# A linear-attention phase re-ordered: maxima and copies of the cross-attention into waits for roots, states ahead of running sums, outputs of two heads in halves

## The chip, the cores and the metric

The kernel runs on one core of a Trainium2 chip. The core has five engines that run side by side, each through its own list of instructions in order, and meet at semaphores: TensorE (PE, matrix products), VectorE (DVE), ScalarE (ACT), GpSimd (POOL) and SyncE (SP, here for issuing transfers). The metric is the device time of one execution in microseconds; lower is better. The median of three timed runs is given, and one further execution was recorded by the profiler.

## The reference

Two causal layers over 1024 tokens of width 1024. The change is in the token mixer of the first, a gated linear attention with four heads, and in the cross-attention to 256 memory tokens that runs beside it:

```python
def gla_mixer(h, w_in, w_gate2, b_gate, o_norm):
    q, k, v, glr, og, xq = split_cols(h @ w_in, ...)
    log_a = jax.nn.log_sigmoid((glr @ w_gate2 + b_gate).astype(F32)) / GLA_GATE_NORM
    o = chunked_gla(hs(q) * (GLA_DK ** -0.5), hs(k), hs(v), hs(log_a))
    o = rms_norm(o, o_norm).reshape(Bsz, S, D_MIX) * jax.nn.silu(og.astype(F32))
    return o.astype(h.dtype), xq

def chunked_gla(q, k, v, log_a):                  # chunks of 64 tokens
    b = jnp.cumsum(log_a, axis=2)
    att = jnp.einsum('bnihk,bnjhk->bnhij', q * jnp.exp(b - b_ref), k * jnp.exp(b_ref - b))
    o_intra = jnp.einsum('bnhij,bnjhv->bnihv', jnp.where(tril, att, 0.0), v)
    def step(state, xs):
        o = jnp.einsum('bchk,bhkv->bchv', qc, state)
        state = dc[..., None] * state + jnp.einsum('bchk,bchv->bhkv', kc, vc)
    return o_intra + o_inter

def memory_cross_attention(xq, mem_n, w_kv, q_norm, k_norm):
    p = jax.nn.softmax(jnp.einsum('bshd,bmhd->bhsm', q, k) * (XA_HEAD_DIM ** -0.5), axis=-1)
    return jnp.einsum('bhsm,bmhd->bshd', p, v)
```

## The kernel before

Everything is one program in phases: projections, the attention phase here (`gla_phase`), its output projection, a gated MLP, and then a second layer of other kind. At the end of a phase the engines meet at a barrier. Only `gla_phase` is touched. In it each engine has a list written out by hand, head after head; nothing else decides the order.

In a head `h` PE projects the head's queries and keys (`project`: weights split into a high and a low part, eight pieces over the width, each of six products), makes the gate (`gate`), the token products inside pairs of chunks and across a pair (`token_products`), turns the keys (by the identity) and makes the state changes from them (`state_changes`), and last the outputs (`outputs`, from the attention and from the state, eight pairs of chunks). In heads 0 and 1 the projections of the next head lie between; heads 2 and 3 have no such work, and there the cross-attention lies between, in 19 steps. A step `s` (class `CrossUnits`) makes on PE the score of unit `s` (L1996), turns the weights of unit `s - 2` (L2004) and mixes the values of unit `s - 3` (L2013). DVE makes the maximum of the score (L2021), copies the turned weights out of PSUM (L2029), inverts the total, and scales the mixed values (L2036). ACT makes the exponentials (L2048, two of 256 columns). Each waits for the one before it, and score `s` needs the exponentials of `s - 2`, since two banks take turns. The table `CROSS` says at which place of which head the steps stand, the same for the three engines:

```python
CROSS = {(1, "out"): range(0, 3), (2, "att"): range(3, 5), (2, "state"): range(5, 8), (2, "out"): range(8, 11),
         (3, "att"): range(11, 13), (3, "state"): range(13, 16), (3, "out"): range(16, CrossUnits.STEPS)}
```

DVE further makes the running sums of the log gates (`sums_of`: the log, L2371; a scan, L2372; two differences), four products of queries and keys with the gate factors (`product`, 0 to 3), a pair of factors after the cross products (`cross_pair`), the seven states one after the other (`states`, L2427 and L2429) and the scaled outputs (`outputs`, L2438). The outputs need the reciprocal root of their mean square: ACT squares each pair's output (L2350), POOL makes the root for four pairs at once (L2244, L2246). "Root" below means this chain. ACT also copies the attention, the turned keys (L2333) and the projections (`copy`) out of PSUM, makes the softplus of the gate (`gate_in`, `gate_out`), the gate's factors (`factor`) and the high parts of weights (`high`); DVE makes their low parts (`low`, L2366). Four PSUM banks are handed on as a ring: each use waits until the use four places earlier has been read.

## Time and profile before

| | us |
|---|---|
| median of the timed runs | 2525.84 (2524.62 to 2526.7) |
| profiled execution, its own time | 2521.81 |
| its span, first to last instruction | 2520.0 |
| PE busy | 2432.4 (97%) |
| DVE, ACT, POOL busy | 1729.7, 1033.7, 225.7 |
| mean granted TensorE clock | 0.988 |

The phase runs from 216 to 406 us of the span. In the views below, the table of windows gives for each stretch its length and then each engine's busy time with the number of its instructions, in the order PE, PEld (PE's weight loads), DVE, ACT, POOL, then PEclk, the granted clock of TensorE (1.00 is 2.4 GHz, 0.50 is 1.2 GHz), the share of the transfer engines, and GB/s. A row of a timeline has the start, the duration, the engine, the line of the kernel, the operation, what it writes from what, the shapes, and the number of instructions merged into it; in brackets stand the engine's idle time before it and what ended it. On PE a product in 32 bits counts as two. The end of a matrix product is modelled and overlaps the next start, so the time from one piece of work to the next is read from start to start.

### The profile page before, as it was taken

What the parts mean: (1) busy time and instruction counts of PE and PEld (TensorE: products, weight loads), DVE (VectorE), ACT (ScalarE), POOL (GpSimd) and SP (SyncE); (2) the same over time, 40 slices, a digit from 0 to 9 for tenths busy, and PEclk for the clock granted to TensorE, in tenths of its full rate; (3) what the DMA queues carried; (4) which work ended last, traced back from release to release, by engine and by line L of the source; (5) the groups of instructions that cost most, each with busy time, mean ns of one, the idle gap of its engine ahead of it and who ended that gap; (6) DMA issues with size and microseconds to landing.
All of it is one profiled execution on the core that took longest, in us unless ns stands there. A gap on an engine that the chain in (4) does not pass through costs nothing. (4 is left out here: it accounts for less than half of the span.)

```text
span 2520.0 us, 32372 instructions
## 1 busy us (share of the span) xinstructions
PE 2432.4 (97%) x11700; PEld 2055.1 (82%) x11700; DVE 1729.7 (69%) x2908; ACT 1033.7 (41%) x2126; POOL 225.7 (9%) x271
## 2 busy tenths in 40 slices
PE   7999979999999999998999999999899999999998
PEld 7998757888888887777889889887788888888777
DVE  4532564379899888885553562463669999898896
ACT  6433443344444443335434432333334444443443
POOL 1010021000000000041212021122100000000000
PEclk9999988999999999999999999999999999999999
DMA  4330121322222248743102011212532222226764
GB/s 149 89 89 22 39 79 43 100 69 84 76 92 84 75 142 272 262 142 130 51 17 81 35 34 42 60 34 73 168 115 75 85 84 83 77 91 221 280 200 146
DMA packets 207541, 257.72 MB, mean 102 GB/s; under 512 B 38376, under 2 KB 141784, under 8 KB 207384
## 3 DMA queue, kind: packets, MB, share of 16 engines
q1 hardware_dynamic: 203224, 255.65, 31.0%
q8 instruction: 94, 1.54, 0.3%
q10 hardware_dynamic: 4160, 0.02, 0.1%
q14 instruction: 63, 0.52, 0.1%
HBM read 206.54 MB, written 49.09 MB: 101 GB/s over the span
## 5 line engine op out<-in xcount | busy, mean ns | idle before, releaser
L52 PE MATMUL psum<-f_T_lo 128*128 128x512 f32 x616 | 244.6, 397 | 13.0 <-DVE f_T_lo L676 11.9
L53 PE MATMUL psum<-f_T_lo 128*128 128x512 f32 x616 | 241.3, 392 | 0.0
L54 PE MATMUL psum<-f_T_lo 128*128 128x512 f32 x616 | 241.2, 392 | 0.0
L52 PE MATMUL psum<-w_hi,hT_hi 128*128 128x512 f32 x576 | 229.3, 398 | 4.2 <-DVE w_lo L1445 2.5
L54 PE MATMUL psum<-w_hi,hT_lo 128*128 128x512 f32 x576 | 226.3, 393 | 0.0
L53 PE MATMUL psum<-w_lo,hT_hi 128*128 128x512 f32 x576 | 226.1, 393 | 0.0
L52 PEld LDWEIGHTS psum<-f_T_lo 128*128 128x128 f32 x616 | 116.4, 189 | 48.1 <-DVE f_T_lo L676 21.1
L52 PEld LDWEIGHTS psum<-w_hi,hT_hi 128*128 128x128 f32 x576 | 124.8, 217 | 22.4 <-issue 3.9
L54 PEld LDWEIGHTS psum<-w_hi,hT_lo 128*128 128x128 f32 x576 | 125.0, 217 | 17.9
L53 PEld LDWEIGHTS psum<-w_lo,hT_hi 128*128 128x128 f32 x576 | 125.1, 217 | 16.6
L52 PE MATMUL psum<-hT_hi,f_up_hi 128*128 128x512 f32 x352 | 137.4, 390 | 0.4 <-DVE f_up_lo L615 0.4
L54 PE MATMUL psum<-hT_hi,f_up_lo 128*128 128x512 f32 x352 | 137.0, 389 | 0.0
L53 PE MATMUL psum<-hT_lo,f_up_hi 128*128 128x512 f32 x352 | 137.0, 389 | 0.0
L54 PEld LDWEIGHTS psum<-f_T_lo 128*128 128x128 f32 x616 | 116.4, 189 | 25.0
L53 PEld LDWEIGHTS psum<-f_T_lo 128*128 128x128 f32 x616 | 116.4, 189 | 23.1
L52 PE MATMUL psum<-T_hi,f_s_hi 128*128 128x512 f32 x320 | 124.5, 389 | 0.0
L53 PE MATMUL psum<-f_T_lo,f_s_hi 128*128 128x512 f32 x320 | 124.5, 389 | 0.0
L54 PE MATMUL psum<-T_hi,f_s_lo 128*128 128x512 f32 x320 | 124.5, 389 | 0.0
L52 PE MATMUL psum<-T_hi,f_up_hi 128*128 128x512 f32 x320 | 124.5, 389 | 0.0
L53 PE MATMUL psum<-f_T_lo,f_up_hi 128*128 128x512 f32 x320 | 124.5, 389 | 0.0
L54 PE MATMUL psum<-T_hi,f_up_lo 128*128 128x512 f32 x320 | 124.5, 389 | 0.0
L455 ACT ACTIVATE f_T_lo<-f_up_pieces 128x1024 fp32r<-128x1024 f32 (+1 forms) x72 | 67.0, 957 | 119.1 <-PE psum L54 101.9
(416 smaller groups left out, 6087.7 us busy)
## 6 DMA issues: line engine op xcount, KB each, us to landing
raw<-in_ffn_w_up_dram SPq DMA_DIRECT2D x88, 512.0 KB, 4.7
activations<-f_act SPq DMA_DIRECT2D x44, 512.0 KB, 2.6
f_up_pieces<-activations SPq DMA_DIRECT2D x38, 512.0 KB, 4.4
w_raw<-in_b_w_in_dram SPq DMA_DIRECT2D x18, 1024.0 KB, 5.9
f_up_pieces<-in_ffn_w_down_dram SPq DMA_DIRECT2D x20, 512.0 KB, 4.8
x_between<-XY SPq DMA_DIRECT2D x16, 512.0 KB, 5.2
XY<-x_between SPq DMA_DIRECT2D x16, 512.0 KB, 6.5
f_up_pieces<-activations SPq DMA_DIRECT2D x28, 256.0 KB, 3.9
```

The costliest lines, as they stand in the source:

```text
L52: nc.tensor.matmul(out, lhs_hi, rhs_hi, start=start, stop=False)
L53: nc.tensor.matmul(out, lhs_hi, rhs_lo, start=False, stop=False)
L54: return nc.tensor.matmul(out, lhs_lo, rhs_hi, start=False, stop=stop)
L455: nc.scalar.activation(hi, raw, ACT.Copy).then_inc(b_high, 1)
```

## The change

Only the order of instructions inside `gla_phase` changes, and with it the points at which they wait.

- PE, heads 0 and 1: the keys are turned before the last of the eight pieces of the projection, not after it. The state products, which need ACT's copies of them, follow that piece. ACT takes the copies of the keys first, then the high part of the next weight, then the copy of the projection.
- PE, outputs in two halves, with a new place `half` between them: in head 1 scores 0 and 1 stand there, in head 3 step 16. A new place `keys` stands between the turned keys and the state products: step 5 in head 2, step 13 in head 3.
- DVE, all heads: outputs in two halves; in heads 0 and 1 products 2 and 3 of the next head stand between them.
- DVE, heads 2 and 3, written out one by one: the states of head 2 stand before the scan of head 3; cross steps stand between products and output halves.
- ACT, head 2: the gate factors of head 3 stand between the two halves of the squares; the exponentials of steps 3 and 4 stand ahead of the copies of the keys.

The diff, without the parts that only name the new ring entries:

```diff
-        CROSS = {(1, "out"): range(0, 3), (2, "att"): range(3, 5), (2, "state"): range(5, 8), (2, "out"): range(8, 11),
-                 (3, "att"): range(11, 13), (3, "state"): range(13, 16), (3, "out"): range(16, CrossUnits.STEPS)}
+        CROSS = {(1, "half"): range(0, 2), (1, "out"): range(2, 3), (2, "att"): range(3, 5), (2, "keys"): range(5, 6), (2, "state"): range(6, 8),
+                 (2, "out"): range(8, 11), (3, "att"): range(11, 13), (3, "keys"): range(13, 14), (3, "state"): range(14, 16),
+                 (3, "half"): range(16, 17), (3, "out"): range(17, CrossUnits.STEPS)}
...
@@ scalar engine
-                if fresh:
-                    copy(h + 1, 0)
-                    high(2 * h + 3)
+                cross_steps(cross.act, act, h, "att")
                 if h:
                     act.wait_ge(squared, PAIRS * h)
                 for i in range(2):
                     act.wait_ge(mixed, mixes_before(at(h, "keys", i)) + 1)
                     nc.scalar.activation(k_rows[:, 4 * i:4 * i + 4, :], ...)
-                cross_steps(cross.act, act, h, "att")
-                if more:
+                if fresh:
+                    high(2 * h + 3)
+                    copy(h + 1, 0)
+                cross_steps(cross.act, act, h, "keys")
+                if fresh:
                     factor(h + 1, 0)
                     factor(h + 1, 1)
-                cross_steps(cross.act, act, h, "state")
-                if fresh:
                     copy(h + 1, 1)
                 if h + 2 < LAST:
                     high(2 * h + 4)
+                cross_steps(cross.act, act, h, "state")
                 if h:
                     act.wait_ge(rstd_ready, 2 * h)
                 for p in range(PAIRS):
+                    if p == PAIRS // 2:
+                        if more and not fresh:
+                            factor(h + 1, 0)
+                            factor(h + 1, 1)
+                        cross_steps(cross.act, act, h, "half")
                     act.wait_ge(mixed, mixes_before(at(h, "out", p // 2)) + 1)
...
@@ vector engine (logs_of is the log of sums_of, split off)
-            for h in range(GLA_HEADS):
-                more = h + 1 < GLA_HEADS
-                fresh = h + 1 < LAST
+            for h in range(LAST - 1):
                 cross_pair(h)
-                cross_steps(cross.dve, dve, h, "att")
-                if more:
-                    sums_of(h + 1)
-                if fresh:
-                    low(2 * h + 3)
+                logs_of(h + 1)
+                sums_of(h + 1)
+                low(2 * h + 3)
                 states(h)
...
-                if more:
-                    product(h + 1, 1)
-                outputs(h)
-                if more:
-                    product(h + 1, 2)
-                    product(h + 1, 3)
-                if h == 1:
-                    for part in range(2):
-                        dve.wait_ge(parked[part], 16 * LAST)
-                cross_steps(cross.dve, dve, h, "out")
+                product(h + 1, 1)
+                cross_steps(cross.dve, dve, h, "half")
+                outputs(h, 0)
+                product(h + 1, 2)
+                product(h + 1, 3)
+                outputs(h, 1)
+            for part in range(2):
+                dve.wait_ge(parked[part], 16 * LAST)
+            cross_steps(cross.dve, dve, LAST - 2, "out")
+            first, second, third = CROSS[LAST - 1, "out"]
+            cross_pair(LAST - 1)
+            cross_steps(cross.dve, dve, LAST - 1, "att")
+            cross_steps(cross.dve, dve, LAST - 1, "keys")
+            logs_of(LAST)
+            states(LAST - 1)
+            cross.dve(dve, CROSS[LAST - 1, "state"][0])
+            sums_of(LAST)
+            cross.dve(dve, CROSS[LAST - 1, "state"][1])
+            outputs(LAST - 1, 0)
+            product(LAST, 0)
+            cross.dve(dve, first)
+            product(LAST, 1)
+            outputs(LAST - 1, 1)
+            cross.dve(dve, second)
+            product(LAST, 2)
+            product(LAST, 3)
+            cross.dve(dve, third)
+            cross_pair(LAST)
+            cross_steps(cross.dve, dve, LAST, "att")
+            cross_steps(cross.dve, dve, LAST, "keys")
+            states(LAST)
+            cross_steps(cross.dve, dve, LAST, "state")
+            cross_steps(cross.dve, dve, LAST, "half")
+            outputs(LAST, 0)
+            cross.dve(dve, CROSS[LAST, "out"][0])
+            outputs(LAST, 1)
+            cross.dve(dve, CROSS[LAST, "out"][1])
...
@@ tensor engine (turn_keys is the first half of state_changes, split off)
-                if h + 1 < LAST:
-                    project(2 * h + 2, range(EARLY, DC))
+                fresh = h + 1 < LAST
+                if fresh:
+                    project(2 * h + 2, range(EARLY, DC - 1))
                 cross_at(h, "att")
+                turn_keys(h)
+                if fresh:
+                    project(2 * h + 2, range(DC - 1, DC))
+                cross_at(h, "keys")
                 state_changes(h)
                 cross_at(h, "state")
-                if h + 1 < LAST:
+                if fresh:
                     project(2 * h + 3)
-                outputs(h)
+                outputs(h, 0)
                 if h == 1:
                     pe.wait_ge(copied, 2 * LAST)
                     pe.wait_ge(kv_loaded, 16 * len(kv_loads))
+                cross_at(h, "half")
+                outputs(h, 1)
                 cross_at(h, "out")
```

How this stands in the lists of the engines is shown at three places. The first is PE in head 0, around the turned keys (from `gla_k_out`) and the state products (from `gla_k_rows`); the products with `h_hi` and `h_lo` are the projection. Before:

```order
L2499 MATMUL psum<-h_hi,mem_lo 128x512 x4
L2499 MATMUL psum<-h_lo,mem_lo 128x512 x2
L2499 MATMUL psum<-h_hi,mem_lo 128x512 x2
L2532 MATMUL psum<-ident,gla_k_out 128x96 x8
L2539 MATMUL psum<-gla_v,gla_k_rows 96x192 x7
```

In the changed kernel, whose lines have other numbers, on PE at the same place:

```order
L2536 MATMUL psum<-h_hi,mem_lo 128x512 x2
L2569 MATMUL psum<-ident,gla_k_out 128x96 x8
L2536 MATMUL psum<-h_hi,mem_lo 128x512 x2
L2536 MATMUL psum<-h_lo,mem_lo 128x512 x2
L2536 MATMUL psum<-h_hi,mem_lo 128x512 x2
L2578 MATMUL psum<-gla_v,gla_k_rows 96x192 x7
```

One piece of the projection has moved from before the turned keys to between them and the state products.

The second place is DVE at the end of head 1: the scaled outputs (from `gla_rstd`), the products of head 2 and the first maxima (`rank_rows<-psum`). Before:

```order
L2393 TENSOR_TENSOR gla_k_mid<-XY,gla_k_mid 96x1024
L2438 SCALAR_TENSOR_TENSOR XY<-psum,gla_rstd,XY 128x192 x8
L2402 TENSOR_TENSOR gla_decay<-gla_ends 96x8
L2406 TENSOR_TENSOR gla_k_out<-gla_k_mid,gla_ends 96x1024
L2406 TENSOR_TENSOR gla_q_in<-gla_q_mid,gla_ends 96x1024
L2021 TENSOR_REDUCE rank_rows<-psum 128x2 x3
L2029 COPY cross_room<-psum 128x512
```

In the changed kernel on DVE at the same place:

```order
L2406 TENSOR_TENSOR gla_k_mid<-XY,gla_k_mid 96x1024
L2021 TENSOR_REDUCE rank_rows<-psum 128x2 x2
L2451 SCALAR_TENSOR_TENSOR XY<-psum,gla_rstd,XY 128x192 x4
L2415 TENSOR_TENSOR gla_decay<-gla_ends 96x8
L2419 TENSOR_TENSOR gla_k_out<-gla_k_mid,gla_ends 96x1024
L2419 TENSOR_TENSOR gla_q_in<-gla_q_mid,gla_ends 96x1024
L2451 SCALAR_TENSOR_TENSOR XY<-psum,gla_rstd,XY 128x192 x4
L2021 TENSOR_REDUCE rank_rows<-psum 128x2
L2029 COPY cross_room<-psum 128x512
```

Two of the three maxima have moved ahead of the outputs, and the second four outputs behind the two products; the third maximum still stands behind all outputs.

The third place is DVE in head 2, from the scan (from `gla_keep`) and the states (`gla_state`) to the next cross step. Before:

```order
L2371 SCALAR_TENSOR_TENSOR gla_soft<-raw,gla_soft 96x1024
L2372 SCALAR_TENSOR_TENSOR raw<-gla_keep,gla_soft 96x1024
L2377 TENSOR_TENSOR gla_ends<-raw 96x16
L2378 TENSOR_TENSOR gla_soft<-raw 96x1024
L2427 COPY gla_state<-psum 96x192
L2429 SCALAR_TENSOR_TENSOR gla_state<-gla_state,gla_decay,psum 96x192 x6
L2021 TENSOR_REDUCE rank_rows<-psum 128x2
L2029 COPY gla_v<-psum 128x4x128
```

In the changed kernel on DVE at the same place:

```order
L2382 SCALAR_TENSOR_TENSOR gla_soft<-raw,gla_soft 96x1024
L2440 COPY gla_state<-psum 96x192
L2442 SCALAR_TENSOR_TENSOR gla_state<-gla_state,gla_decay,psum 96x192 x6
L2021 TENSOR_REDUCE rank_rows<-psum 128x2
L2029 COPY cross_room<-psum 128x512
L2030 RECIPROCAL rank_rows<-rank_rows 128x2
L2036 TENSOR_TENSOR XY<-psum,rank_rows 128x128
L2385 SCALAR_TENSOR_TENSOR raw<-gla_keep,gla_soft 96x1024
L2390 TENSOR_TENSOR gla_ends<-raw 96x16
L2391 TENSOR_TENSOR gla_soft<-raw 96x1024
```

The scan and the two differences have moved behind the states and one whole cross step.

## Rows read from the trace of the kernel before

**Rows 1.** PE's waits between 215 and 410 us: total, times, longest.

```profile
PE psum L2004 <- DVE cross_room L2029: 7.0, 2, 4.2
PE psum L1996 <- ACT cross_room L2048: 5.9, 1, 5.9
```

**Rows 2.** Windows: length, busy time of each engine, PEclk, DMA share, GB/s.

```profile
248.15:253.09 4.94, 4.94 (x37) 3.43 (x37) 0.00 (x0) 3.72 (x7) 0.00 (x0) 1.00 0.00 0
324.20:338.30 14.10, 14.08 (x45) 8.43 (x46) 3.30 (x6) 8.74 (x17) 4.96 (x3) 0.50 0.30 125
329.20:338.50 9.30, 9.30 (x38) 6.29 (x37) 1.93 (x4) 6.99 (x9) 0.07 (x2) 0.50 0.00 0
345.70:352.50 6.80, 4.44 (x25) 2.91 (x25) 6.51 (x16) 4.44 (x15) 0.00 (x0) 1.00 0.01 2
367.40:372.80 5.40, 5.32 (x20) 4.21 (x20) 2.54 (x7) 1.47 (x7) 0.00 (x0) 0.50 0.00 0
400.70:405.80 5.10, 4.39 (x21) 4.26 (x21) 1.51 (x5) 0.00 (x0) 0.00 (x0) 0.50 0.00 0
311.50:405.80 94.30, 77.47 (x428) 61.05 (x426) 56.04 (x121) 39.38 (x134) 23.09 (x22) 0.84 0.15 55
```

**Rows 3.** PE's timeline in head 0, up to the next projection.

```profile
253.09 0.72 PE L2499 MATMUL psum<-h_hi,mem_lo 128*128 128x512 f32 x2
...
258.69 0.82 PE L2532 MATMUL psum<-ident,gla_k_out 96*128 96x96 f32 x8
...
261.38 2.49 PE L2539 MATMUL psum<-gla_v,gla_k_rows 128*96 128x192 f32 x14 [1.87 <-ACT gla_k_rows L2333]
...
263.57 0.76 PE L2499 MATMUL psum<-h_hi,mem_lo 128*128 128x512 f32 x2
```

**Rows 4.** DVE's timeline there: the low part of the next weight.

```profile
261.00 1.21 DVE L2366 TENSOR_TENSOR mem_lo<-kv_room,mem_lo 128x1024 fp32r<-128x1024 f32 x1
```

**Rows 5.** PE's timeline: outputs of head 1 and first cross scores.

```profile
311.53 0.81 PE L2551 MATMUL psum<-gla_v,gla_att 128*128 128x192 f32 x4
...
316.43 1.88 PE L1996 MATMUL psum<-kv_room,xqT 128*128 128x512 f32 x4
...
324.22 2.08 PE L1996 MATMUL psum<-kv_room,xqT 128*128 128x512 f32 x2 [5.91 <-ACT cross_room L2048]
```

**Rows 6.** ACT's timeline there: last square of head 1, first exponential.

```profile
316.95 0.32 ACT L2350 ACTIVATE gla_k_rows<-psum 128x192 f32<-128x192 f32 x1
...
323.15 0.47 ACT L2048 ACTIVATE cross_room<-psum,rank_rows 128x256 f32<-128x256 f32 x1 [5.78 <-DVE rank_rows L2021]
```

**Rows 7.** DVE's timeline there: second four outputs, a product, two maxima.

```profile
318.78 1.39 DVE L2438 SCALAR_TENSOR_TENSOR XY<-psum,gla_rstd,XY 128x192 f32<-128x192 f32 x4 [1.23 <-POOL gla_rstd L2246]
...
320.16 1.21 DVE L2406 TENSOR_TENSOR gla_k_out<-gla_k_mid,gla_ends 96x1024 f32<-96x1024 f32 x1
...
322.43 1.28 DVE L2021 TENSOR_REDUCE rank_rows<-psum 128x2 f32<-128x512 f32 x2
```

**Rows 8.** Timelines of DVE, then PE: sums, states and cross steps of head 2.

```profile
343.56 2.29 DVE L2372 TENSOR_TENSOR_SCAN raw<-gla_keep,gla_soft 96x1024 f32<-96x1024 f32 x1
...
347.12 0.35 DVE L2427 COPY gla_state<-psum 96x192 f32<-96x192 f32 x1
...
350.78 0.68 DVE L2029 COPY gla_v<-psum 128x512 f32<-128x512 f32 x1
...
351.61 0.63 PE L2004 MATMUL psum<-ident,cross_room 128*128 128x128 f32 x4 [1.56 <-DVE gla_v L2029]
...
352.91 1.08 PE L1996 MATMUL psum<-kv_room,xqT 128*128 128x512 f32 x2
...
355.10 0.87 PE L2551 MATMUL psum<-gla_v,gla_att 128*128 128x192 f32 x4
```

**Rows 9.** Timelines of DVE and PE where one phase ends and the next begins.

```profile
405.18 0.29 DVE L2036 TENSOR_TENSOR XY<-psum,rank_rows 128x128 f32<-128x128 f32 x1 [1.41 <-PE psum L2013]
...
405.80 1.94 PE L1317 MATMUL psum<-ident,XY 128*128 128x128 f32 x8 [0.65 <-PEq L2064]
```

More of the change, by code:

```diff
@@ L2162, in gla_phase @@
             enter("keys", "act", 2, h)
+            enter_cross(h, "keys")
             enter("delta", "state", 4, h)
             enter_cross(h, "state")
-            enter("out", "dve", 4, h)
+            enter("out", "dve", 2, h)
+            enter_cross(h, "half")
+            enter("out_end", "dve", 2, h)
             enter_cross(h, "out")
@@ L2184, in at @@
         def at(h, kind, i=0):
+            if kind == "out" and i >= 2:
+                return entry_of[h, "out_end"] + i - 2
             return entry_of[h, kind] + i
@@ L2431, in states, with outputs @@
                     dve.wait_ge(state_ready, (PAIRS - 1) * h + p + 1)
-            def outputs(h):
-                for p in range(PAIRS):
+            def outputs(h, half):
+                for p in range(half * PAIRS // 2, (half + 1) * PAIRS // 2):
                     if p % (PAIRS // 2) == 0:
-                        dve.wait_ge(rstd_ready, 2 * h + 1 + p // (PAIRS // 2))
+                        dve.wait_ge(rstd_ready, 2 * h + 1 + half)
                     y = Y[:, p, h * DV:(h + 1) * DV]
@@ L2443, in _ @@
             dve.wait_ge(kept, 2)
+            logs_of(0)
             sums_of(0)
@@ L2449, in _ @@
             product(0, 3)
-            for h in range(GLA_HEADS):
-                more = h + 1 < GLA_HEADS
-                fresh = h + 1 < LAST
+            for h in range(LAST - 1):
                 cross_pair(h)
-                cross_steps(cross.dve, dve, h, "att")
-                if more:
-                    sums_of(h + 1)
-                if fresh:
-                    low(2 * h + 3)
+                logs_of(h + 1)
+                sums_of(h + 1)
+                low(2 * h + 3)
                 states(h)
-                cross_steps(cross.dve, dve, h, "state")
-                if more:
-                    product(h + 1, 0)
+                product(h + 1, 0)
@@ L2463, in _ @@
                 if h + 2 < LAST:
                     low(2 * h + 4)
-                if more:
-                    product(h + 1, 1)
-                outputs(h)
-                if more:
-                    product(h + 1, 2)
-                    product(h + 1, 3)
-                if h == 1:
-                    for part in range(2):
-                        dve.wait_ge(parked[part], 16 * LAST)
-                cross_steps(cross.dve, dve, h, "out")
+                product(h + 1, 1)
+                cross_steps(cross.dve, dve, h, "half")
@@ L2524, in token_products, with turn_keys @@
                 mm.then_inc(mixed, 1)
-            def state_changes(h):
+            def turn_keys(h):
                 pe.wait_ge(factored, h + 1)
@@ L2533, in state_changes @@
                     mm.then_inc(mixed, 1)
+            def state_changes(h):
                 for p in range(PAIRS - 1):
@@ L2542, in state_changes, with outputs @@
                         mm.then_inc(mixed, 1)
-            def outputs(h):
+            def outputs(h, half):
                 pe.wait_ge(masked, h + 1)
-                for p in range(PAIRS):
+                for p in range(half * PAIRS // 2, (half + 1) * PAIRS // 2):
                     i = at(h, "out", p // 2)
```

3 lines of the change are left out of this document (2 added, 1 removed).

## The prediction, made before the changed kernel was run

> **What bounds the kernel now.** I read the waits of TensorE (PE) first. The kernel is PE's: over most of it PE runs without a gap, and only one stretch, the gated linear attention from 216 to 406 us, which the change touches, has large waits: 5.9 us once before a cross-attention score, 4.2 and 2.8 us before turns of the weights [rows 1], and 1.87 us in each of heads 0 and 1 before the state products [rows 3]. Then I read the granted clock. After each of the three long waits PE is granted 0.50, its lower level of 1.2 GHz, and stays there for 14.08, 5.32 and 4.39 us of busy time; the other stretches of the table have 1.00 [rows 2]. At half rate these cost half their busy time, 11.9 us. So from the outputs of head 1 to the end of the phase, 311.5 to 405.8, 94.3 us are 77.5 busy [rows 2], of which 65.6 would be left at full rate, 11.9 for the low clock, and 16.8 of waiting. These last two are what a new order can win: 28.7 us, beside 3.7 in heads 0 and 1.
>
> **Why PE waits there.** The 5.91 us before 324.22 [rows 5]: PE has made scores 0 and 1, and score 2 needs ScalarE's (ACT) exponentials of score 0, which need VectorE's (DVE) maximum. DVE, in order, first finishes head 1: it waits for the root, scales four outputs from 318.78, makes two products, and reaches the maxima at 322.43 [rows 7]; the exponentials start 0.72 later and score 2 1.07 after that [rows 5, 6]. The 4.2 and 2.8 us are the same at heads 2 and 3: a copy of turned weights stands behind the root, the outputs and, in head 2, the products.
>
> **Heads 0 and 1.** The keys are turned at 258.69, ACT first has a copy and a weight part to do, and the state products start at 261.38 [rows 3]. After, the keys are turned one piece of projection earlier. Four pieces take 5.60 (253.09 to 258.69), one 1.4, so they are turned at 257.3, take 0.8, and the last piece fills PE to 259.5, while ACT, now with the keys first, has copied them by 258.8. State products: 259.5 to 261.7 (2.19). The next projection needs the low weight part, which DVE still makes at 261.00 behind the running sums, 1.2 long [rows 4]; ACT gives its high part by 260.7, so that doesn't delay it. PE starts at about 262.3 in place of 263.57. A 1.87 wait goes, one of 0.6 comes: **1.29 us per head, 2.6 for two.** ACT's copy of the projection moves behind the weight part and ends at 261.6, still before PE asks for it; SP's store of it stands behind a load that waits for the low part anyway. DVE's second four outputs now come two products, 2.4 us, later; PE has half a projection and a gate, 5.6 and 1.9, to do before it wants their banks: nothing, and at most 2.4 each if that cover were gone.
>
> **Head 1 into head 2**, on the old time axis less 2.6. Outputs take 4.90 [rows 5]: first half 308.95 to 311.2, scores 0 and 1 to 313.1, second half to 315.7. DVE takes the maximum of score 0 at 312.4, ACT the exponentials at 313.1, so they are out at 314.15, before PE asks for them at 315.7. The wait of 5.91 is gone, and with it the fall of the clock behind it. What is late next: the second root. The last squares start at 316.2, DVE's outputs 1.83 later [rows 6, 7] at 318.0, the maximum of score 2 behind them at 319.35, its exponentials at 320.1 to 321.0, and behind these, in order on ACT, the gate of head 3, whose first two activations (1.4) free the bank that PE's last token products want. PE has turned weights 0 and made gate and token products, 4.94 us together with the last [rows 2], and stands there at 320.9: a wait of 1.5.
>
> **Heads 2 and 3.** A full step of cross-attention is 2.19 of PE, and DVE needs 0.64 for a maximum (two in 1.28 [rows 7]) and about as much for a copy, 0.83 from a copy's start to the next turn [rows 8]; so DVE keeps pace unless something stands in front of it. I walked the new order with these lengths; the waits left on PE:
> - 1.2 us at score 5: ACT ends gate, two attention copies, the softplus and its table loads (6.99 busy in the like stretch [rows 2]) before the exponentials of step 3, now ahead of the key copies; they start at 328.95, PE stands at 328.9.
> - 0.8 at turn 5: seven states and a maximum, 3.66 together (347.12 to 350.78 [rows 8]), stand before the copy of step 6. The states now precede the scan, 3.56 with what follows it [rows 8], so the scan no longer holds them up; it delays step 7 instead, 0.4 at the outputs of head 2.
> - 0.9 at mix 5: step 7's exponentials end at 343.6, the four squares behind them at 345.0, so DVE's first root comes at 346.4 and the bank at 347.15.
> - 1.35 at turn 7 behind one product (1.2 [rows 7]), and 1.7 at turn 8 behind the second product and four outputs (1.39).
> - 1.15 in four small ones, the largest 0.5 at the outputs of head 3, which wait for the first root there.
> - 1.95 at the end: PE is done at 381.7, DVE's last outputs, behind the root of the last squares, at 383.05, the last cross output at 383.35, and the next phase 0.3 later, as 405.80 stands to 405.47 now [rows 9].
>
> Together with the 1.5: 10.95 us. None is longer than 1.7. Gaps of 1.87 in heads 0 and 1 left the clock at 1.00, and so did 345.7 to 352.5, where PE is busy for 4.44 of 6.80 us [rows 2]; the gaps before a fall were 2.8 and more. So I take no fall before the end of the phase. Cold start of the next phase: as before.
>
> One rule of the Trainium skill speaks against this. Its page "TensorE: Matmul & The Clock Gate", section "A second HAM failure mode: psum-queue depth-cycling", says that a PE which idles often for short times between groups of products can swing between both rates and pay again and again. By it the sum would be that of the first rival below. This trace doesn't agree in the one like stretch it has, just named.
>
> **Sum.** Before: 65.6 + 16.8 + 11.9 = 94.3. After by this balance: 65.6 + 10.95 = 76.5, a gain of 17.8, with heads 0 and 1 20.4. Walked from start to start, the phase ends at 383.65 in place of 405.80, a gain of 22.15: the balance counts as work the drain of the last product before each of nine waits, some 0.2 each, and the walk forgets small delays. I take the middle, **21.3 us**. Against the profiled execution, 2521.81, that is 2500.5. The median of the timed runs is 4.0 above it, 2525.84, and becomes **2504.5**. No instruction is added or taken out, table loads included; only the order differs.
>
> **Rivals.**
> 1. *The clock falls in the new gaps* (0.25). The weakest place is 343 to 354, four gaps of 4.3 us together and the engine about half busy, sparser than the one stretch that kept its clock. For: the three falls now each followed a sparse stretch; against: each had one gap of 2.8 or more. Price: the three low stretches cost 7.0, 2.7 and 2.2 us now; the new waits would swallow 1 or 2 of it. One fall costs 2 to 6, two up to 9: 2506.5 to 2513.5. The rule of the Trainium skill's page named above would give this.
> 2. *Waits I counted too short* (0.06): ACT is in order, and the squares of head 2 stand behind exponentials of step 7. If the scan comes a step late, root, outputs and copies of three steps follow, each 1 to 3 us: gain of 12 to 15, 2511 to 2514.
> 3. *The change doesn't reach the wait* (0.03): the half outputs ask for the copies of the projection and the loaded keys before score 0. If one of them is late, the 5.9 stays. Against it: the copy ends at about 310.2, the keys land long before. Then only heads 0 and 1 are won: 2523, same.
> 4. *Slower* (0.03): PE falls to half rate at the first new gap and the sparse order never lets it rise. Some 54 us of the 65.6 of work come after that point; at half rate they take 54 more, of which the waits left, 9, are covered. It decides from the point where the low rate lasts for more than some 30 us of work (21 won and 9 covered); held to the end it costs 45 and gives 2549.5. Against it: the longest low stretch now is 14.1 us, and work of the same kind ended it.
>
> **Numbers.** 0.63 for the forecast, with a range of its own of 2502 to 2507 (balance and walk, and small delays). Beyond about 0.2%, 5 us, a time can be told from no change here. Forecast, rival 1 and rival 2 are all faster by more: 0.94; the same 0.03; slower 0.03. The range runs from 2501, the walk's 2503.7 less what a warmer start of the next phase could save of its first work (1.94 at low clock [rows 9] and what follows), to 2512, most of rival 1, leaving out about 0.15.
>
> **What would show it.** In the changed profile: no wait over 2 us on PE between 311 and 380, granted clock 1.00 throughout; state products of heads 0 and 1 without a wait, the projection after them waiting 0.6 for DVE; exponentials of score 0 between the squares of head 1; waits of 1 to 2 us at the cross token products of head 2, at score 5, and at turns 7 and 8; the next phase's first PE instruction near 383.7. It is wrong if the clock shows 0.50 anywhere there, if a gap exceeds 3 us, or if the phase ends after 390.

## The result, and the profile after the change

The changed kernel's median is 2504.84 us (9 runs, 2496.31 to 2511.73), that of the kernel before 2523.99 in the same session (9 runs): a ratio of 0.9928, with a 95% interval of 0.9915 to 0.9941. Its profiled execution took 2497.09, with a span of 2495.3 and a mean granted clock of 0.992. The phase runs from its first PE instruction at 216.91 to the next phase's at 385.70, 168.79 long; before it was 188.64 (217.16 to 405.80 [rows 9]), so 19.85 were won in it. The other 5 of the profile's difference lie outside it, and runs of one kernel differ by more than that (below).

PE's waits in the phase (total, times, longest), which answer to [rows 1]:

```profile
PE psum L2004 <- DVE gla_v L2029: 2.5, 2, 1.5
...
PE psum L2004 <- DVE cross_room L2029: 1.6, 2, 1.0
...
PE psum L2536 <- DVE mem_lo L2378: 1.2, 3, 0.4
PE psum L2013 <- DVE XY L2451: 1.0, 1, 1.0
PE psum L2554 <- DVE XY L2451: 0.6, 1, 0.6
```

The 5.9 at a score is gone, and the 4.2 and 2.8 at turns with it; inside the phase no wait is longer than 1.5, and 1.77 stands at its end. The windows from head 1's outputs to the end, around the token products of head 2, and over head 2's outputs answer to [rows 2] (columns as there):

```profile
308.64:385.70 77.06, 68.93 (x427) 55.30 (x426) 57.22 (x121) 38.39 (x134) 23.82 (x22) 0.96 0.18 68
319.24:326.36 7.12, 6.96 (x35) 5.41 (x35) 3.54 (x6) 5.96 (x12) 6.26 (x4) 0.54 1.02 416
346.78:357.40 10.62, 7.14 (x44) 4.80 (x43) 9.06 (x21) 5.65 (x23) 2.66 (x4) 1.00 0.00 1
```

PE's busy time fell from 77.47 to 68.93 because less of it is at half rate. One fall of the clock is left, at 319.24, where the prediction has none; over 346.78 to 357.40, where its first rival saw the weakest place, PE works 7.14 of 10.62 us and the clock is 1.00. PE's timeline, in head 0 (as [rows 3]), from head 1's outputs into head 2 (as [rows 5]) and at the end (as [rows 9]):

```profile
257.08 0.82 PE L2569 MATMUL psum<-ident,gla_k_out 96*128 96x96 f32 x8
...
259.16 2.44 PE L2578 MATMUL psum<-gla_v,gla_k_rows 128*96 128x192 f32 x14
262.02 0.74 PE L2536 MATMUL psum<-h_hi,mem_lo 128*128 128x512 f32 x2 [0.42 <-DVE mem_lo L2378]
...
308.64 0.81 PE L2590 MATMUL psum<-gla_v,gla_att 128*128 128x192 f32 x4
...
310.92 1.88 PE L1996 MATMUL psum<-kv_room,xqT 128*128 128x512 f32 x4
...
319.24 3.19 PE L2554 MATMUL psum<-gla_q_mid,gla_k_mid 96*128 96x128 f32 x16 [0.65 <-DVE XY L2451]
322.59 1.97 PE L2559 MATMUL psum<-gla_q_in,gla_k_out 96*64 96x64 f32 x16 [0.16 <-ACT gla_soft L2284]
...
329.91 0.63 PE L2004 MATMUL psum<-ident,cross_room 128*128 128x128 f32 x4 [1.03 <-DVE gla_v L2029]
...
385.70 1.07 PE L1317 MATMUL psum<-ident,XY 128*128 128x128 f32 x8 [1.77 <-PEq L2064]
```

State products start without a wait, and the next projection waits 0.42 for the low part. The 1.03 at 329.91 was not predicted. What made it stands in the timelines of POOL and DVE there:

```profile
311.94 0.19 POOL L2251 TENSOR_SCALAR gla_sums<-gla_sums 128x4 f32<-128x4 f32 x1 [20.25 <-ACT gla_k_rows L2362]
...
316.27 0.95 POOL L2251 TENSOR_SCALAR gla_sums<-gla_sums 128x4 f32<-128x4 f32 x1 [3.05 <-ACT gla_k_rows L2362]
...
324.47 2.35 POOL L1118 TENSOR_TENSOR h_lo<-o_w_stage,h_hi 128x1024 fp32r<-128x1024 f32 x1
...
315.96 1.21 DVE L2419 TENSOR_TENSOR gla_q_in<-gla_q_mid,gla_ends 96x1024 f32<-96x1024 f32 x1
...
324.60 2.77 DVE L2430 TENSOR_TENSOR gla_q_in<-gla_q_in,gla_ends 96x512 f32<-96x512 f32 x1 [3.58 <-PE psum L2559]
```

DVE's product at 324.60 takes 2.77; the same line takes 0.69 in other heads. It ends 0.55 after POOL's split of the output weights (326.82), nearly as if it had only started there. And POOL's first step of the second root takes 0.95 in place of 0.19: it ends at 317.22, 0.05 after DVE's product does.

### The profile page after: what moved, and what is told of

Its sections match the earlier page's. It is cut to its first block and busy times, and to the rows that moved or that the text cites. A ratio compares the mean times of both kernels' runs of the same rounds, so it can differ in the third digit from the quotient of the medians.

```text
span 2495.3 us, 32379 instructions
## 1 busy us (share of the span) xinstructions
PE 2423.2 (97%) x11700; PEld 2049.3 (82%) x11700; DVE 1731.1 (69%) x2908; ACT 1033.1 (41%) x2126; POOL 226.0 (9%) x271
```

## The experiments

Three stretches tell the kernels apart: from the phase's first PE instruction to head 1's outputs, from there to head 2's outputs, and from there to the next phase. They are differences of start times in PE's timeline of each profile; falls are the places in the phase at which the granted clock drops to 0.50 (0 to 3: in that head; 1 into 2: between its outputs and the next head's products).

| kernel | to head 1's outputs | to head 2's outputs | to the next phase | phase | falls (head) |
|---|---|---|---|---|---|
| before | 94.37 | 43.57 | 50.70 | 188.64 | 1 into 2, 2 into 3, end |
| changed | 91.73 | 32.86 | 44.20 | 168.79 | 2 |
| early keys alone | 91.64 | 40.20 | 50.25 | 182.09 | 1 into 2, 2, 2 into 3, end |
| halves alone | 96.03 | 37.01 | 50.66 | 183.70 | 0, 2, 2 into 3, end |
| sums ahead of states | 91.69 | 37.42 | 45.65 | 174.76 | 2 (twice), 3 |
| head 3 uncut | 91.67 | 32.39 | 47.53 | 171.59 | end |
| changed, again | 91.68 | 32.45 | 47.19 | 171.32 | 2, 3 |
| splits moved | 91.72 | 31.43 | 44.20 | 167.35 | none |
| product behind | 94.59 | 36.27 | 44.19 | 175.05 | 0, 2 (twice) |
| splits and product | 94.50 | 30.65 | 47.16 | 172.31 | 1, 3 |
| splits moved, again | 91.73 | 31.62 | 44.20 | 167.55 | 2 |
| gate twice | 106.78 | 32.56 | 44.19 | 183.53 | start, 0, 1, 2 |
| filler | 93.56 | 31.42 | 45.06 | 170.04 | none |
| gate early | 91.76 | 31.58 | 44.19 | 167.53 | 2 |

**Early keys alone**, on the kernel before:

```diff
-                    project(2 * h + 2, range(EARLY, DC))
+                    project(2 * h + 2, range(EARLY, DC - 1))
                 cross_at(h, "att")
-                state_changes(h)
+                turn_keys(h)
+                if h + 1 < LAST:
+                    project(2 * h + 2, range(DC - 1, DC))
+                state_changes(h)
```

(on ACT the key copies come first, then the weight part and the copy, as in the change)

> The kernel before with one part of the change: in heads 0 and 1 PE turns the keys one piece ahead of the end of the projection, and ACT copies them ahead of the weight part and of the projection's copy. Theory (the term of 1.29 per head): the wait of 1.87 before the state products goes, one of about 0.5 for VectorE's low weight part comes; head 1's outputs start 2.6 us earlier than the 311.53 of before, and all that follows keeps its length, the 5.9 wait included. Median about 2.6 below before, 2521. Rival: the low part decides alone when the next projection starts, and nothing is won: outputs start at 311.5. Rival: the key copies moved ahead delay the weight's high part and the low part with it, and it is slower by up to 1 per head.

Ratio 0.9989 (0.998 to 0.9999). Head 1's outputs come 2.73 earlier; both rivals fall. What follows is not as long as before, though its order is the same: PE's timeline at the 5.9 wait, and the windows behind it:

```profile
321.64 2.07 PE L1996 MATMUL psum<-kv_room,xqT 128*128 128x512 f32 x2 [5.90 <-ACT cross_room L2048]
```

```profile
321.66:325.00 3.34, 3.34 (x7) 1.75 (x8) 1.09 (x2) 1.36 (x7) 3.31 (x2) 0.51 1.02 418
325.00:344.00 19.00, 16.15 (x103) 11.34 (x101) 14.21 (x28) 14.29 (x31) 3.44 (x2) 1.00 0.06 24
```

The same wait cost 3.34 of work at half rate here, and 14.08 in the profile of before [rows 2]. How long a fall lasts is not fixed by the order.

**Halves alone**, on the kernel before:

```diff
-        CROSS = {(1, "out"): range(0, 3), (2, "att"): ...
+        CROSS = {(1, "half"): range(0, 2), (1, "out"): range(2, 3), (2, "att"): ...
...
                     product(h + 1, 1)
+                cross_steps(cross.dve, dve, h, "half")
                 outputs(h)
```

(PE makes these two steps, and ACT their exponentials, between the two halves of head 1)

> The kernel before with another part alone: head 1's outputs in two halves with scores 0 and 1 between them on PE, their two maxima ahead of the scaling of outputs on VectorE, their exponentials between the squares on ACT; heads 2 and 3 keep their order. Theory A (the wait is gone, and with it the low clock behind it): no wait of more than 1.5 between head 1's outputs and the scores of head 2, score 2 follows the second half without a wait; 5.9 of wait and 7.0 of low clock go, 1 to 1.5 of small waits come: the later waits and clock falls of heads 2 and 3 stay, and the phase ends some 11.5 earlier than 405.8, at 394. Theory B (as in the trace of the changed kernel, where the clock falls behind the gate's products all the same): the clock is granted 0.50 for some 6 us from the token products of head 2 on, and the phase ends some 8.5 earlier, at 397.3. Rival: what was won at the scores is waited for at the next turn of the weights, and less than 4 is left.

Ratio 0.9992 (0.9981 to 1.0004): not to be told from no change. In the profile the second stretch is 6.56 shorter, between theory B (8.5) and the last rival (4): the wait at the score is gone, but a new one stands at the cross token products (waits of PE, 308 to 345):

```profile
PE psum L2525 <- ACT gla_soft L2277: 3.6, 1, 3.6
```

They need a bank that ACT's gate frees, which stands behind the exponentials of score 2; their maximum comes after the outputs and two products of 1.2 on DVE. The changed kernel has these products between the halves, where DVE waits for the root anyway. The clock fell in head 0 too, over the state products (window), behind the same wait of 1.87 that left it at 1.00 before [rows 3]:

```profile
260.95:264.87 3.92, 3.92 (x15) 3.56 (x15) 2.73 (x6) 3.86 (x7) 0.00 (x0) 0.58 0.52 120
```

**Sums ahead of states**, on the changed kernel:

```diff
             logs_of(LAST)
+            sums_of(LAST)
             states(LAST - 1)
             cross.dve(dve, CROSS[LAST - 1, "state"][0])
-            sums_of(LAST)
```

> The changed kernel with one part undone: in head 2 VectorE makes the running sums and their differences (about 3.5 us) ahead of the states again, not behind them and one step of the cross-attention. Theory: states and the step behind them come some 3 later, PE waits there for 2 to 3 more (turn 5 or the outputs), of which the later wait for step 7, 0.99 in the changed kernel, gives some back: the phase is 1.5 to 3 longer than in the changed kernel, 387 to 389 in place of 385.7. Rival: VectorE has the same work to do before step 7 in either order, PE waits there in the end, and the phase is the same within 0.5.

Ratio 0.9945 (0.993 to 0.9961). PE's timeline shows the wait, at mix 3, and the window what came with it:

```profile
340.25 1.54 PE L2013 MATMUL psum<-kv_room,gla_v 128*128 128x64 f32 x8 [2.39 <-DVE gla_state L2442]
```

```profile
340.25:347.60 7.35, 7.15 (x27) 5.60 (x28) 5.13 (x13) 2.04 (x8) 0.00 (x0) 0.54 0.01 3
```

The wait, 2.39, is as long as the theory has it, though two places earlier than turn 5. The second stretch is 4.56 longer than in the changed kernel, not 1.5 to 3: the clock falls behind this wait as well. The later waits are shorter for it. From score 6 to head 3's token products the waits add up to 4.52 (2.39, 0.20, 0.42, 1.51), in the changed kernel to 4.12 (0.64, 0.99, 0.98, 1.51), and the way takes 24.27 in place of 21.05: of the 3.22 more, 0.40 is waiting and the rest is work at half rate. So the rival, by which PE waits as long in either order, is not refuted; what the profile shows is that one long wait in place of short ones was followed by a fall. In the last stretch 1.45 more is lost: a fall in head 3, which came in the unaltered kernel too (below), less the waits at mix 5 and turn 7, shorter by 1.55.

**Head 3 uncut**, on the changed kernel:

```diff
-                 (3, "half"): range(16, 17), (3, "out"): range(17, CrossUnits.STEPS)}
+                 (3, "out"): range(16, CrossUnits.STEPS)}
...
             outputs(LAST, 0)
-            cross.dve(dve, CROSS[LAST, "out"][0])
             outputs(LAST, 1)
-            cross.dve(dve, CROSS[LAST, "out"][1])
+            cross_steps(cross.dve, dve, LAST, "out")
```

> The changed kernel with one part undone: head 3's outputs are no longer cut in two; the step of the cross-attention that stood between the halves follows all of them, on PE, ACT and VectorE. Theory: the copy that turn 15 needs then stands behind VectorE's last outputs, which wait for the root of the last squares; PE waits 2 to 3 there, and the end of the phase is 1.5 to 3 later than the changed kernel's 385.7. Rival: the phase ends when VectorE's last outputs are scaled in either order, and PE's end moves under that: within 0.5. Rival: the wait at the end is 2.8 or more and the clock falls before the next phase, where it is low at the start already: nothing further.

Ratio 0.9943 (0.9926 to 0.996). The last stretch is 3.33 longer: 2.79 of wait, and work at half rate behind it. Up to head 3 this is the changed kernel, and here the clock did not fall in head 2. PE's timeline, and the window of those products:

```profile
319.57 2.02 PE L2553 MATMUL psum<-gla_q_mid,gla_k_mid 96*128 96x128 f32 x16 [0.65 <-DVE XY L2451]
322.92 1.15 PE L2558 MATMUL psum<-gla_q_in,gla_k_out 96*64 96x64 f32 x16 [1.32 <-ACT gla_soft L2284]
...
383.84 1.09 PE L2004 MATMUL psum<-ident,cross_room 128*128 128x128 f32 x4 [2.79 <-DVE cross_room L2029]
```

```profile
319.57:326.24 6.67, 5.34 (x47) 4.56 (x47) 3.91 (x7) 5.51 (x12) 6.00 (x4) 1.00 1.03 421
```

At full rate PE waits 1.32 where the changed kernel's profile has 0.16, and 2.45 at turn 2 where that has 1.03; head 2's outputs come only 0.47 sooner. The fall in the changed kernel lay over time in which PE would have waited.

**The changed kernel again**, unaltered.

> The changed kernel once more, unaltered, to see what its one fall of the clock is worth and whether it comes back. In its first profile the clock is granted 0.50 from the token products of head 2 (behind a gap of 0.65) for 6 us; the kernel with head 3 uncut has the same order up to there and kept 1.00. Theory: the fall is not tied to the order, and beneath it PE waits for VectorE anyway, so that from the first outputs of head 1 to those of head 2 it is 32.4 to 32.9 with or without it, and the phase from its first PE instruction to the next phase's 168.8 within 0.5. Rival: a fall there costs 2 or more, and a run without it is that much shorter.

Ratio 0.9925 (0.9911 to 0.9939). The theory holds for head 2 (32.45, with the fall), not for the phase: 171.32, because the clock fell once more, in head 3, with no wait of over 1.5 ahead of it. The two windows:

```profile
319.35:326.60 7.25, 6.86 (x35) 5.30 (x36) 3.66 (x6) 6.10 (x12) 6.72 (x4) 0.56 0.97 397
355.80:366.00 10.20, 10.20 (x59) 8.50 (x60) 7.53 (x15) 3.33 (x12) 1.83 (x2) 0.67 0.01 2
```

Nothing covers that one: the last stretch is 2.99 longer than in the first profile.

**Splits moved**, on the changed kernel:

```diff
-        SPLITS = {(1, "rstd"): range(0, 2), (3, "mask"): range(2, 4)}
+        SPLITS = {(2, "mask"): range(0, 1), (3, "mask"): range(1, 4)}
```

> The changed kernel with GpSimd's splits of the output weights, which stood behind head 1's roots, moved to where VectorE has no operation with two inputs from the on-chip memory: one chunk behind head 2's mask, the other three behind head 3's. Theory (VectorE's product of 0.69 takes 2.77 because it stands still while a split runs on GpSimd): both products of the cross pair take 0.69, the copy for turn 2 comes some 2 earlier, and the wait of 1.03 there goes; the phase is 1 to 1.6 shorter, 167.2 to 167.8 from its first PE instruction to the next phase's, where the changed kernel has 168.8. Rival: the product is slow for another reason (its own inputs), it stays at 2.5 or more, and nothing changes. Rival: ACT's exponentials of step 3 hold PE in place of the copy, and less than 0.5 is won.

Ratio 0.9917 (0.9903 to 0.9931); phase 167.35, as the theory has it. DVE's timeline, then PE's:

```profile
324.15 0.69 DVE L2430 TENSOR_TENSOR gla_q_in<-gla_q_in,gla_ends 96x512 f32<-96x512 f32 x1 [2.76 <-PE psum L2559]
...
322.97 1.15 PE L2559 MATMUL psum<-gla_q_in,gla_k_out 96*64 96x64 f32 x16 [1.33 <-ACT gla_soft L2284]
...
330.74 1.12 PE L1996 MATMUL psum<-kv_room,xqT 128*128 128x512 f32 x2 [1.22 <-ACT cross_room L2048]
```

The product takes 0.69 with the splits away, the wait at turn 2 is gone, and what holds PE next is score 5, for ACT's exponentials. The first rival falls; the second is right about what comes next, not about the size.

**Product behind**, on the changed kernel: the last product for head 2 goes behind the third step of the cross-attention.

```diff
                 product(h + 1, 2)
-                product(h + 1, 3)
+                if h == 0:
+                    product(h + 1, 3)
                 outputs(h, 1)
...
             cross_steps(cross.dve, dve, LAST - 2, "out")
+            product(LAST - 1, 3)
```

> The changed kernel with VectorE's last product for head 2 (1.21) moved from ahead of head 1's second outputs to behind the third step of the cross-attention; GpSimd's splits stay where they are. Theory (VectorE's product and GpSimd's instructions shut each other out): GpSimd's first step of the second root, 0.95 in the changed kernel beside that product, takes 0.19, the root and the second outputs come 0.75 earlier, and PE's 0.65 wait before the token products goes; but the product then meets GpSimd's splits, takes 2 to 3.5 in place of 1.21, and the cross token products, which need it, come 0.5 to 2 later: phase 168.8 to 170.5. Rival: the two engines do not shut each other out; the root's 0.95 stays, the product takes 1.21, and the phase is the same within 0.5.

POOL's and DVE's timelines:

```profile
319.57 0.19 POOL L2251 TENSOR_SCALAR gla_sums<-gla_sums 128x4 f32<-128x4 f32 x1 [3.05 <-ACT gla_k_rows L2362]
...
323.89 3.21 POOL L1118 TENSOR_TENSOR h_lo<-o_w_stage,h_hi 128x1024 fp32r<-128x1024 f32 x1
...
328.55 2.83 DVE L2431 TENSOR_TENSOR gla_k_out<-gla_k_out,gla_ends 96x512 f32<-96x512 f32 x1
```

The root's first step is back at 0.19, the 0.65 wait gone, and the product itself took 1.42; DVE's next products took 1.49 and 2.83 beside the splits, and POOL's splits 3.21 and 2.68 in place of 2.35. The two hold each other up, whichever starts second. The profile's phase, 175.05, is above what was expected, by falls in head 0 (2.9) and twice in head 2; the timed runs, 0.9914 (0.99 to 0.9928), are as the changed kernel's in the same set (0.9925). The fall in head 0 has no wait in the phase's stretch before it but one of 0.34 nearly 8 us earlier (window):

```profile
250.00:259.00 9.00, 9.00 (x44) 7.61 (x44) 3.92 (x4) 6.33 (x9) 1.10 (x1) 0.62 0.00 0
```

**Splits and product**: both edits.

> Both edits together: the splits moved away, and the product behind the third step. Theory: the root's first step takes 0.19, the product 1.21, second outputs, maximum and exponentials of score 2, gate and cross token products all come 0.75 earlier; with the copy for turn 2 earlier by 2 or more, the phase is 1.5 to 2.4 shorter than the changed kernel's 168.8, and the median about 2 below it. Rival: what is won up to turn 2 is waited for at turn 5 or mix 5 behind the states, and no more than 0.5 is left.

The second stretch is 30.65, 2.21 shorter than the changed kernel's and 0.78 shorter than with the splits moved alone: what the theory has. But the clock fell in heads 1 and 3 (2.8 and 3.0 lost), and the ratio is 0.9934 (0.9921 to 0.9947). Whether this order makes falls likelier stays open: its six runs have a granted clock of 0.989 to 0.992, the five with the splits moved alone 0.990 to 0.994.

The last four ask what the clock falls behind; all have the splits moved.

**Splits moved, again**, unaltered.

> The changed kernel with GpSimd's splits moved, once more and unaltered, as the base for the three kernels beside it and to see whether its profile without a fall of the clock was chance. Theory (falls come by chance behind the gate's and token products of any head, about one in three of those places in the traces so far, at some 2.9 each where nothing covers them): 167.4 from the phase's first PE instruction to the next phase's with no fall, 170.3 with one in head 0, 1 or 3; median 2498 to 2502. Rival: without GpSimd's splits in the way there is no fall, and each profile shows 167.4 within 0.3.

Ratio 0.9905 (0.989 to 0.992), phase 167.55, with a fall in head 2 that cost 0.19 there. So the profile without a fall was chance, and the rival falls.

**Gate twice**:

```diff
                     nc.tensor.matmul(bank(i)[0:DK, :], gate2[:, h * DK:(h + 1) * DK], rank[:, half * HALF:(half + 1) * HALF],
+                                     start=True, stop=True)
+                    nc.tensor.matmul(bank(i)[0:DK, :], gate2[:, h * DK:(h + 1) * DK], rank[:, half * HALF:(half + 1) * HALF],
                                      start=True, stop=True).then_inc(z_ready, 1)
```

> The changed kernel with the splits moved, and each of the gate's two products made twice into the same bank, which adds 1.88 of PE work ahead of the token products in each of heads 0, 1 and 2. Theory (the gate's products ahead of the token products are what the clock falls behind): a fall to 0.50 in at least two of these three heads; the phase is 167.4 + 5.0 of added work (in head 2 the wait of 0.66 covers a part) + 2.9 for each fall in heads 0 and 1: 175 to 179. Rival (falls have nothing to do with the gate): none or one, 172.4 to 175.

**Filler**:

```diff
             def token_products(h):
                 pe.wait_ge(timed, 4 * h + 2)
+                if h < LAST - 1:
+                    for d in range(4):
+                        nc.tensor.matmul(psum[:, 2, :], first_parts.hi[0][:, d, :], hT_hi[:, d, 0:HALF], start=True, stop=True)
+                else:
+                    nc.tensor.matmul(psum[:, 2, :], xqT[:, 0, 0:P], keys[:, 0:2, :].rearrange("p h n -> p (h n)"), start=True, stop=True)
```

> The changed kernel with the splits moved, and unneeded products of full size between the gate and the token products of each head, into a bank that nobody reads: four of the projection's kind (0.23 each) in heads 0 and 1, one score (0.86) in heads 2 and 3. Theory: with full products between, the clock stays at 1.00 in all four heads; the phase is 167.4 + 0.9 in each of heads 0, 1 and 3 and 0.2 to 0.9 in head 2: 170.3 to 171. Rival: falls as before, one or two in four heads, each 2.9 more: 173 to 176.

Windows around the products in question, first with the gate twice (the first gate of the phase, then heads 0, 1 and 2):

```profile
225.00:230.00 5.00, 5.00 (x12) 2.96 (x11) 0.00 (x0) 4.25 (x6) 0.00 (x0) 0.67 0.00 0
254.00:265.00 11.00, 11.00 (x47) 9.57 (x47) 5.10 (x5) 5.73 (x7) 1.10 (x1) 0.53 0.00 0
294.00:305.00 11.00, 11.00 (x44) 8.05 (x43) 2.65 (x4) 6.99 (x9) 0.78 (x1) 0.55 0.00 0
335.00:343.00 8.00, 8.00 (x42) 6.37 (x41) 3.51 (x8) 7.67 (x14) 0.82 (x1) 0.57 0.67 274
```

then with the filler (heads 0 to 3):

```profile
250.00:260.00 10.00, 10.00 (x68) 8.62 (x68) 5.13 (x5) 6.86 (x10) 1.10 (x1) 1.00 0.00 1
285.00:296.00 11.00, 11.00 (x70) 8.67 (x69) 4.59 (x5) 7.76 (x11) 1.10 (x1) 1.00 0.01 1
318.00:328.00 10.00, 8.84 (x58) 6.06 (x57) 6.05 (x12) 5.79 (x13) 2.35 (x3) 1.00 0.91 373
356.00:366.00 10.00, 9.51 (x72) 7.54 (x72) 8.64 (x19) 4.07 (x15) 2.14 (x3) 1.00 0.01 2
```

With the gate twice the clock falls at every gate of the phase, in the last of its products or behind it, in stretches where PE is busy without a gap (11.00 of 11.00). The phase, 183.53, is longer than the 175 to 179 expected, since the phase's first gate is doubled too (1.88 more, which the expectation forgot), the clock fell behind it as well, and each fall lasted longer. With the filler it falls nowhere, and the phase is 170.04, the 2.7 of added work longer than the base. Ratios: 0.9962 (0.9948 to 0.9975) and 0.9922 (0.9909 to 0.9935). The timed runs bear out what the profile shows of the gate: with it twice all six have a granted clock of 0.987 to 0.989, the base's five 0.992 to 0.994, and the median is 13.5 above the base's for 7.5 of added work (four gates at 1.88). They do not bear out the filler: its granted clocks, 0.991 to 0.994, are no higher than the base's, and the median is 4.1 above the base's for 2.7 of added work. No fall in the four places of its one profile could be chance. In the eight profiles of the changed order above that have the gate once, the clock fell at the token products in 7 of 24 places with a gate ahead (heads 0 to 2) and in 3 of 8 without one (head 3). So more of the gate's work makes a fall likelier, but a fall doesn't need the gate, and that full products prevent one is not shown.

**Gate early**: the gate's products of heads 1 and 2 one piece of projection earlier.

```diff
                 if h + 2 < LAST:
-                    project(2 * h + 4, range(EARLY))
+                    project(2 * h + 4, range(EARLY - 1))
+                    gate(h + 2)
+                    project(2 * h + 4, range(EARLY - 1, EARLY))
```

(and the same ahead of head 0)

> The changed kernel with the splits moved, and the gate's products of heads 1 and 2 made one piece of projection earlier, so that in heads 0 and 1 a full piece of projection (1.4) stands between them and the token products; no work is added. Theory: falls in heads 0 and 1 go, a phase of 167.4 with none in heads 2 and 3 and 170.3 with one in head 3; the median is equal to the base's or up to 1 below it. Rival: the falls are tied to the token products alone and stay. Rival: the earlier gate waits for its banks, and heads 0 or 1 are 0.5 or more longer.

No fall in heads 0, 1 and 3, one in head 2, where the order is the base's; no bank is waited for (91.76). Ratio 0.9911 (0.9899 to 0.9924), between the base's two. The base had no fall in heads 0 and 1 either, so one profile does not settle what this is worth.

## Why the prediction was right, and where it was not

**Waits.** Heads 0 and 1 were worth 2.64, and alone 2.73, for 2.6; the new wait there is 0.42 for 0.6. Scores 0 and 1 between the halves do away with the 5.9, as walked. The small waits of heads 2 and 3 came nearly where they were put: 0.64 at turn 5 (0.8), 0.99 at mix 5 (0.9), 0.98 at turn 7 (1.35), 1.51 at turn 8 (1.7), 0.33 at head 3's outputs (0.5), 1.77 at the end (1.95). Where the clock is full, the 1.5 at the cross token products became two waits, 0.65 before the token products and 1.33 before the last of them, and the 1.2 at score 5 is 1.22 once turn 2 no longer hides it.

**A missing term: POOL.** The step "DVE's outputs 1.83 later", from the last squares of head 1, took its length from rows in which DVE was idle beside the root. The change puts a product there, and the step took 2.58 (315.77 to 318.35). The trace of before had the price, in head 0 (timelines of POOL, then DVE):

```profile
278.31 0.93 POOL L2244 TENSOR_SCALAR gla_sums<-gla_sums 128x4 f32<-128x4 f32 x1 [21.97 <-ACT gla_k_rows L2350]
...
277.97 1.22 DVE L2393 TENSOR_TENSOR gla_k_mid<-XY,gla_k_mid 96x1024 f32<-96x1024 f32 x1
```

There too POOL's step took 0.93 beside a product and ended 0.05 after it; it cost PE nothing there, and the walk passed over it. Further on, DVE's product of the cross pair stood behind POOL's split. Moving both out of the way won 2.21 in that stretch, the splits alone 1.43; with the splits moved the phase is 167.35, 21.29 shorter than before (167.55 and 21.09 in a second profile). That this is the predicted 21.3 so nearly is in part luck: it is measured against a single profile of before, whose falls could have been shorter (see the balance below), and the root's first step still takes 0.96 in it. The Trainium skill has the rule, on the page "SBUF — State Buffer", section "SBUF: two separate sides": a VectorE operation with two inputs in the on-chip memory and a GpSimd operation that reads from it shut each other out, and the one that starts first keeps the shared ports to its end. The trace agrees: 2.77 against 0.69 beside a split, 0.95 against 0.19 beside a product.

**The clock: the step that failed.** The reading "the gaps before a fall were 2.8 and more. So I take no fall before the end of the phase" does not hold. The clock fell behind a gap of 0.65, and in other runs behind none; the same 1.87 in head 0 left it at 1.00 in one kernel and not in another. By the prediction's own sign, a clock of 0.50 anywhere between 311 and 380, its mechanism is wrong here, though no wait is over 2 and the phase ends at 385.70. The clock falls at the gate's and token products in some executions and not in others; what decides which stays open. The forecast was close all the same, since the one fall of the profile lay over waits. Rival 1 named a clock that falls in the new gaps, at 343 to 354; there it stayed at 1.00, so its place was wrong. The rule that the prediction weighed (the Trainium skill, "TensorE: Matmul & The Clock Gate", section "A second HAM failure mode: psum-queue depth-cycling") is not borne out by this stretch: 7.14 busy of 10.62 us there, in short pieces, at 1.00. Falls at the token products, at about one place in three and 2.8 to 3.0 each where no wait covers them, are the term that it put at nothing.

**The balance.** The 11.9 of low clock was read from one execution; with the same 5.9 wait another had 3.34 of busy time at half rate in place of 14.08. A gain taken from such a stretch is a sample, not a price. The walk, which needs no such figure, had 22.15 for a measured 19.85; the collision with the splits (1.4) makes up most of the difference.

**The median.** 2504.5 was forecast, 2504.84 measured, and 2500.54 in a second session. The three runs that the forecast started from, median 2525.84, lay above the median of all nine of their set, 2523.99, so the medians are 19.15 apart, and 19.16 in the second session (2519.70 to 2500.54), not 21.3. Runs follow the clock: over 41 runs of the kernel before in the later sets, the time falls by 2.0 us for each 0.001 of mean granted clock (a straight line through them), and a spread of 3.2 (standard deviation) shrinks to 1.5 about that line. That the median agrees within 0.4 is luck: a base 1.85 too high offset a gain 2.15 too large.

**A version that may be faster still** is the change with the splits moved: 0.9917 and 0.9905 of the time before in two sets, where the changed kernel has 0.9928 and 0.9925. The intervals overlap, so the times don't show it; the phase is 1.2 to 1.4 shorter in both profiles than in the first of the changed kernel.

## What to carry to other kernels

When an order of work changes, look at what each moved operation will stand beside, not only at what it waits for: a VectorE product of two inputs from memory next to GpSimd's work can cost four times its length, and the profile of before shows it only where the two meet: here at places where it cost PE nothing. A fall of the clock is an event of an execution: compare stretch by stretch, profile a kernel twice before a few microseconds are put down to an edit, and see whether the granted clocks of the timed runs say the same. A wait that goes matters only as far as the next one in line; walk on until nothing is late.

## What the runs showed of the hardware

The granted clock fell to 0.50 in stretches where PE had no gap: at gate and token products in head 0 (0.62 over 9.00 busy of 9.00 us), at the token products of head 3, which have no gate ahead (0.67 over 10.20 of 10.20), and at all four gates when each was made twice. With some 0.9 us of full products ahead of the tokens it stayed at 1.00 in four heads of four in the one profile, but the timed runs had no higher clock. A single fall at these places cost 2.8 to 3.0 where PE was the bound, and 0.1 to 0.5 in head 2, where it would have waited anyway. DVE and POOL held each other up in both directions: 2.77 and 2.83 for 0.7 on DVE, 0.95 for 0.19 and 3.21 for 2.35 on POOL.
